# Queries of latent attention projected for two heads and two token tiles a step

## The reference, cut to what matters

```python
def mla_mixer(h, positions, w_in, q_a_norm, kv_a_norm, w_q_b, w_kv_b, q_norm, k_norm, w_out):
    b, s, _ = h.shape
    proj = h @ w_in
    cq = rms_norm(proj[..., :Q_LORA], q_a_norm)                     # 384 wide
    ckv = rms_norm(proj[..., Q_LORA:Q_LORA + KV_LORA], kv_a_norm)   # 256 wide
    k_rope = proj[..., Q_LORA + KV_LORA:]                           # 32 wide, one for all heads
    q = (cq @ w_q_b).reshape(b, s, MLA_HEADS, QK_DIM)               # 64 nope + 32 rope a head
    kv = (ckv @ w_kv_b).reshape(b, s, MLA_HEADS, QK_NOPE + V_DIM)   # 64 key + 64 value a head
    q_nope, q_rope = q[..., :QK_NOPE], q[..., QK_NOPE:]
    k_nope, v = kv[..., :QK_NOPE], kv[..., QK_NOPE:]
    q_nope = rms_norm(q_nope, q_norm[:QK_NOPE])
    q_rope = rms_norm(q_rope, q_norm[QK_NOPE:])
    k_nope = rms_norm(k_nope, k_norm[:QK_NOPE])
    k_rope = rms_norm(k_rope, k_norm[QK_NOPE:])
    cos, sin = rope_cos_sin(positions)
    q_rope = apply_rope(q_rope, cos[:, :, None], sin[:, :, None])   # x1*cos - x2*sin, x2*cos + x1*sin
    k_rope = apply_rope(k_rope, cos, sin)
    o = causal_block_attention(q_nope, q_rope, k_nope, k_rope, v)
    return o.reshape(b, s, MLA_HEADS * V_DIM) @ w_out
```

## Time and profile before

| | |
|---|---|
| Median of 3 runs | 2739.85 us (2738.59 to 2742.94) |
| The profiled execution's own time | 2739.83 us |
| Its span in the trace | 2738.6 us |
| TensorE busy | 2669.8 us, 97% of the span |
| DVE, ScalarE, POOL busy | 1608.3, 857.6, 665.7 us |
| Chain that ended last, by engine | PE 31%, DVE 5%, ACT 2%, issue 1%, POOL 1%, DMA 1% |

### The profile page before, as it was taken

The page is one execution under the profiler, slowest core; times in us unless marked ns, Lnnn a source line. Parts: engine busy times, 40 slices in busy tenths (PEclk is TensorE's granted clock), DMA queues, the critical chain, the costliest instruction groups (busy, mean ns, idle before and its releaser), DMA issues. The chain is left out here.

```text
span 2738.6 us, 33114 instructions
## 1 busy us (share of the span) xinstructions
PE 2669.8 (97%) x12932; PEld 2200.0 (80%) x12932; DVE 1608.3 (59%) x2366; ACT 857.6 (31%) x1485; POOL 665.7 (24%) x726
## 2 busy tenths in 40 slices
PE   8999999999999999999999999999999999899998
PEld 7888887787778888888888789878888878777776
DVE  5343468888746545555455556644443467768875
ACT  2101126676511001111011245521001035537885
POOL 2111121221321211221111258712111131012220
PEclk9999999999999999999999999999999999999999
DMA  4333333333235435444354400023333454048995
GB/s 126 98 95 100 93 98 110 94 104 95 79 102 152 140 114 145 117 137 140 115 147 130 151 17 1 1 72 98 99 94 100 93 68 72 8 140 287 349 357 218
DMA packets 456847, 325.84 MB, mean 119 GB/s; under 512 B 34434, under 2 KB 420819, under 8 KB 456435
## 3 DMA queue, kind: packets, MB, share of 16 engines
q1 hardware_dynamic: 434568, 282.77, 35.4%
q10 hardware_dynamic: 15498, 32.54, 3.7%
q0 software_dynamic: 6624, 8.41, 0.9%
HBM read 323.06 MB, written 16.32 MB: 124 GB/s over the span
## 5 line engine op out<-in xcount | busy, mean ns | idle before, releaser
L254 PE MATMUL bank<-h_hi,w_hi 128*128 128x512 f32 x1992 | 790.2, 397 | 8.9 <-DVE w_lo L246 4.4
L256 PE MATMUL bank<-h_hi,w_lo 128*128 128x512 f32 x1992 | 776.2, 390 | 0.0
L255 PE MATMUL bank<-h_lo,w_hi 128*128 128x512 f32 x1992 | 775.8, 389 | 0.0
L232 POOL TENSOR_SCALAR w_hi<-w_lo_exact 128x1024 fp32r<-128x1024 f32 x325 | 358.1, 1102 | 1483.0 <-DMA w_lo_exact<-in_ffn_w_gate 386.3
L246 DVE TENSOR_TENSOR w_lo<-w_lo_exact,w_hi 128x1024 fp32r<-128x1024 f32 x369 | 454.9, 1234 | 143.0 <-POOL w_hi L232 131.3
L254 PEld LDWEIGHTS bank<-h_hi,w_hi 128*128 128x128 f32 x1992 | 374.3, 188 | 95.5 <-ACT h_hi L350 6.8
L255 PEld LDWEIGHTS bank<-h_lo,w_hi 128*128 128x128 f32 x1992 | 374.5, 188 | 79.6 <-issue 3.6
L256 PEld LDWEIGHTS bank<-h_hi,w_lo 128*128 128x128 f32 x1992 | 374.2, 188 | 79.0
L254 PE MATMUL bank<-g_hi,w_hi 128*128 128x512 f32 x704 | 273.9, 389 | 0.0
L255 PE MATMUL bank<-g_lo,w_hi 128*128 128x512 f32 x704 | 273.9, 389 | 0.0
L256 PE MATMUL bank<-g_hi,w_lo 128*128 128x512 f32 x704 | 273.9, 389 | 0.0
(11 more groups left out here) (492 smaller groups left out, 3873.3 us busy)
## 6 DMA issues: line engine op xcount, KB each, us to landing
w_lo_exact<-in_ffn_w_gate SPq DMA_DIRECT2D x88, 512.0 KB, 3.8
w_lo_exact<-in_ffn_w_up SPq DMA_DIRECT2D x88, 512.0 KB, 3.9
w_lo_exact<-in_ssm_w_in SPq DMA_DIRECT2D x48, 512.0 KB, 4.1
mod_w<-in_w_mod ACTq DMA_DIRECT2D x48, 512.0 KB, 3.8
e_lo_exact<-in_w_gate SPq DMA_DIRECT2D x46, 512.0 KB, 5.7
e_lo_exact<-in_w_up SPq DMA_DIRECT2D x46, 512.0 KB, 6.7
e_lo_exact<-in_w_down SPq DMA_DIRECT2D x46, 512.0 KB, 5.9
w_lo_exact<-in_ffn_w_down SPq DMA_DIRECT2D x32, 512.0 KB, 4.0
```

The source lines that it names most:

```text
L232: ge.tensor_scalar(k.w_hi[:, u % SLOTS, :], k.raw[:, u % SLOTS, :], 1.0, 0.0, ALU.mult, ALU.add).then_inc(*k.up("w hi", u))
L254: te.matmul(k.bank[bank][:, :], hi, x_hi, start=first, stop=False)
L255: te.matmul(k.bank[bank][:, :], hi, x_lo, start=False, stop=False)
L256: return te.matmul(k.bank[bank][:, :], lo, x_hi, start=False, stop=stop)
```

## The change

Five edits in the latent attention stage:

- A query projection no longer covers one head and four token tiles, but two heads and two token tiles: six products of 192 columns in place of twelve of 96. There are still 16 of them, called s here; s = 0 and 1 are heads 0 and 1 (tiles 0 and 1, then 2 and 3), s = 2 and 3 heads 2 and 3, and so on. A head needs both of its pair's, so queries run one step further ahead: in step h, s = h+3. The lead-in does s = 0, 1 and 2. The normalised queries have two buffers, the second in a slot of the weight ring, whose load (the fourth unit of the projection out) waits until the last query is turned.
- The gains of the query's and key's nope part become one column, their product. It multiplies the query when it is turned: ScalarE's high part takes it as a scale, DVE's low part as the scalar of a SCALAR_TENSOR_TENSOR. Two DMAs of 96 single elements load it.
- The gains of the query's rope part go into four copies of the rotation's tables, `turns`, made once by POOL (`mla_tables_pool`, eight instructions).
- POOL's two gain multiplications a head (L2048, L2049) are gone; its rotation stays.
- Sums and normalisation run over i = -1 to 15: index i handles the key of head i and the query projection i+1.

```diff
@@ mla_tiles
+    k.base = k.ring_at + late_out_unit(k) % SLOTS * UNIT * 4
+    k.qc.append(sb("qc", [P, NT, 2, QK]))
+    k.turns = k.nr[:, :].rearrange("p (n a c) -> p n a c", n=4, a=2 * NT)
+    k.q_banks = [by_tile(k.bank[b][:, 0:NT * QK], NT) for b in (0, 3)]
@@ mla_sync
     for u in range(k.unit_at["mla"], k.unit_at["ffn11"]):
+        if u == late_out_unit(k):
+            k.se.wait_ge(*k.at("turned q", MLA_HEADS - 1))
         load_unit(k, u)
@@ mla_tensor
-    mla_project_tensor(k, 0, "q")
+    mla_queries_tensor(k, 0)
     te.wait_ge(*k.at("latent scaled", ("kv_a", LK - 1)))
-    mla_project_tensor(k, 0, "kv")
+    mla_keys_tensor(k, 0)
     mod_sum_tensor(k, 4, 14)
-    mla_project_tensor(k, 1, "q")
-    mla_project_tensor(k, 1, "kv")
+    mla_queries_tensor(k, 1)
+    mla_queries_tensor(k, 2)
+    mla_keys_tensor(k, 1)
     mla_turn_tensor(k, 0)
@@ in the loop over h
         if h + 2 < MLA_HEADS:
-            mla_project_tensor(k, h + 2, "q")
-            mla_project_tensor(k, h + 2, "kv")
+            if h + 3 < MLA_HEADS:
+                mla_queries_tensor(k, h + 3)
+            mla_keys_tensor(k, h + 2)
@@
+def mla_queries_tensor(k, s):
+
+    te = k.te
+    if s >= 2:
+        te.wait_ge(*k.at("normal", (s - 2, "q")))
+    for t in range(2):
+        tt, out = 2 * (s % 2) + t, q_bank(k, s)[:, 2 * t:2 * t + 2, :].rearrange("p a b -> p (a b)")
+        for m in range(LQ):
+            ins = te.matmul(out, k.latent[:, m, span(tt)], k.wq[:, m, s // 2 * 2 * QK:(s // 2 + 1) * 2 * QK], start=m == 0, stop=m == LQ - 1)
+    ins.then_inc(*k.up("projected q", s))
@@ mla_turn_tensor
-        te.wait_ge(*k.at(name + "c", h))
+        if name == "k":
+            te.wait_ge(*k.at("normal", (h, "kv")))
+            te.wait_ge(*k.at("kc", "rope"))
+        else:
+            te.wait_ge(*k.at("qc", h // 2 * 2 + 1))
@@ mla_scalar, lead-in
+    for n, name in enumerate(("mla_q_norm", "mla_k_norm")):
+        ae.dma_start(k.gain_col[:, n:n + 1], d[name].rearrange("a h -> h a")).then_inc(*k.up("load gain columns", "all", 16))
...
     mla_query_scalar(k, 0)
+    mla_inverse_scalar(k, -1, 2 * NT, NOPE)
+    mla_query_scalar(k, 1)
     mla_keys_scalar(k, 0)
     mla_inverse_scalar(k, 0, 3 * NT, NOPE)
-    mla_query_scalar(k, 1)
+    mla_query_scalar(k, 2)
     mla_keys_scalar(k, 1)
@@ mla_turn_scalar
-        ae.copy(t[:, 0, :], k.bank[TURN_BANKS[b]][0:QK, :]).then_inc(*k.up(name + "t hi", h))
+            ae.activation(t[:, 0, :], k.bank[TURN_BANKS[b]][0:QK, :], ACT.Copy, scale=k.gain_col[:, 2:3]).then_inc(*k.up("qt hi", h))
@@ mla_turn_vector
+            ve.scalar_tensor_tensor(t[:, 1, :], k.bank[TURN_BANKS[b]][0:QK, :], k.gain_col[:, 2:3], t[:, 0, :].bitcast(F32), ALU.mult, ALU.subtract).then_inc(*k.up("qt lo", h))
@@ mla_sums_vector
+    ve, s = k.ve, i + 1
+    if i >= 0:
+        ve.wait_ge(*k.at("sq k", i))
+    ve.wait_ge(*k.at("rr", i - 1 if s else "k rope"))
+    if s < MLA_HEADS:
+        ve.wait_ge(*k.at("sq q", s))
...
@@ mla_normalise_vector
+    ve.wait_ge(*k.at("rr", i))
+    if s < MLA_HEADS:
+        if s >= 4:
+            ve.wait_ge(*k.at("turned q", s // 2 * 2 - 3))
...
+    if i >= 1:
+        ve.wait_ge(*k.at("turned k", i - 1))
@@ mla_normalise_pool, gone
-    ge.tensor_tensor(k.qc[:, :, :], k.qc[:, :, :], k.gain[:, 0, :].unsqueeze(1).broadcast_to([P, NT, QK]), ALU.mult).then_inc(*k.up("qc", (h, 0)))
-    ge.tensor_tensor(k.kc[:, :, 0:NOPE], k.kc[:, :, 0:NOPE], k.gain[:, 1, 0:NOPE].unsqueeze(1).broadcast_to([P, NT, NOPE]), ALU.mult).then_inc(*k.up("kc", h))
```

More of the change, by code:

```diff
@@ L1868, in mla_vector @@
     mla_frequencies_vector(k)
+    mla_gain_vector(k)
     ve.wait_ge(*k.at("inverse rms", "mla"))
@@ L1891, in mla_vector @@
     mla_scaled_vector(k, "kv_a", LQ, LK)
-    for h in range(2):
-        mla_sums_vector(k, h)
-        if h:
+    for i in range(-1, 2):
+        mla_sums_vector(k, i)
+        if i == 1:
+            ve.wait_ge(*k.last("gain column"))
             mla_turn_vector(k, 0)
-        mla_normalise_vector(k, h)
+        mla_normalise_vector(k, i)
     for h in range(MLA_HEADS + 1):
@@ L1937, in mla_scaled_vector, with mla_gain_vector @@
         ve.scalar_tensor_tensor(k.latent[:, k0 + m, :], k.latent[:, k0 + m, :], k.col(name, m), k.latent_r[name], ALU.mult, ALU.mult).then_inc(*k.up("latent scaled", (name, m)))
+def mla_gain_vector(k):
+    ve = k.ve
+    ve.memset(k.gain_col[NOPE:QK, 2:3], 1.0).then_inc(*k.up("gain column", 0))
+    ve.wait_ge(*k.at("load gain columns", "all"))
+    ve.tensor_tensor(k.gain_col[0:NOPE, 2:3], k.gain_col[0:NOPE, 0:1], k.gain_col[0:NOPE, 1:2], ALU.mult).then_inc(*k.up("gain column", 1))
 def mla_frequencies_vector(k):
@@ L2017, in mla_pool @@
     split_pool(k, u0 + LQ + LK + 1, u0 + LQ + LK + 3)
-    mla_rotate_pool(k, k.kr[:, :, :], k.kc[:, :, NOPE:QK], "kc", "rope", k.at("unit", u0 + LQ + LK))
+    mla_rotate_pool(k, k.kr[:, :, :], k.kc[:, :, NOPE:QK], [t[:, :, :] for t in (k.cos, k.sin, k.cos, k.sin)], "kc", "rope")
+    mla_tables_pool(k)
     for half in range(2):
@@ L2021, in mla_pool @@
             fill_pool(k, values[:, half, :, n, :], 0.0, "vn")
-    mla_normalise_pool(k, 0)
-    mla_normalise_pool(k, 1)
+    for s in range(3):
+        mla_queries_pool(k, s)
     for h in range(MLA_HEADS):
```

119 lines of the change are left out of this document (69 added, 50 removed).

## The result

The changed kernel takes 2741.19 us (median of 14 runs, 2738.22 to 2744.73), the kernel before beside it 2739.35 (2736.03 to 2742.94). The ratio is 1.0014, interval 1.0007 to 1.0020: slower by a small amount, where 2738.0 and "no change" were forecast. The profiled execution took 2743.49 us, 2742.2 of it the span.

What follows compares the result with a forecast made beforehand. TensorE, busy 97% of the span, was taken as the bound. 2739.83 + 6.8 (lead-in) + 0.4 (DMAs) - 7.4 (steps 0 to 12) - 1.6 (step 13) = 2738.0 us; own range 2735 to 2741, 8 in 10 2733.5 to 2743.

Steps and rivals of the forecast that it cites:

- The pass: Loop's query projections: a 192-column pass takes 0.168 us, twelve take 2.01 us, gaining 0.64 us a projection.
- the line between 128 and 512: Interpolation between float32 passes of 128 columns (0.114 us) and 512 (0.4375 us), giving 0.168 us for 192.
- The gain column: Loop steps: DVE's low part of the query, now with a column, takes 0.07 us more, paid each step.
- step 13: Loop step carrying only keys now: falls from 11.26 us to about 9.7, 1.6 us less.
- The lead-in: Ahead of the loop: TensorE waits about 3.3 us before query 2; head 0 starts 6.8 us late, slow clock included.
- The clock term: Lead-in: clock falls at the 3.3 us stop, low until about 1606, losing 2.8 us; bounds 0 and 4.2.
- The two cases of the earlier trace: TensorE waits of 3.50 and 2.53 us in this stage, both with the clock falling from 2.4 to 1.2 GHz.
- low for long: Rival, lead-in: clock stays low 10.2 us as in the second earlier case, 1.4 us more, 2739.4 us; chance 13%.
- The DMAs: Stage's start: two more DMAs on ScalarE ahead of `wq` and `wkv` add 0.4 us, bounds 0 and 0.9.
- Clock stays up: Rival, lead-in: the clock does not fall at the stop, 2.8 us less, 2735.2 us; chance 15%.
- step not shorter: Rival, loop: step stays 11.27 us as another wait, likeliest ScalarE's weights and squares, replaces PE's work; 2745.4 us; chance 7%.
- pass not cheaper: Rival, loop: a 192-column pass takes 0.221 us, as two of 96, so nothing is gained; 2746.3 us; chance 5%.

Runs made afterwards that it cites:

- pad_late: Changed kernel with already met waits on TensorE's queue in the experts' stage behind the mixer (368 more instructions): 2737.69 us, ratio 0.9995.
- pad128: Changed kernel with already met waits on TensorE's queue in the feed-forward stage ahead of the mixer (114 more instructions by the page): 2736.22 us, ratio 0.9994.
- after: The changed kernel as first measured against the kernel before: 2741.19 us, ratio 1.0014.
- after_again: The changed kernel once more, unchanged: 2742.01 us, ratio 1.0009 to the kernel before.
- early_q1: Changed kernel with query projection 1 issued directly behind query projection 0, ahead of the keys: 2736.17 us, ratio 0.9986.
- before: The kernel without the change, timed beside the changed one: 2739.35 us.
- before_again: The kernel before once more, unchanged, as a control: 2737.84 us, ratio 0.9998.
- before_pad128: Kernel before with the same already met waits in the feed-forward stage ahead of the mixer: 2737.84 us, ratio 0.9998.
- before_short: Kernel before without the third product of each expert's gate and up projection (368 instructions, behind the mixer); leaves work out, no time given; mixer 157.0 us.
- nogain_late: The kernel padded by 368 instructions in the experts' stage, with the nope gain column left out of what is computed: 2738.56 us, ratio 1.0000.
- pad_long: Changed kernel with more met waits on TensorE's queue in the experts' stage (736 more instructions by the page): 2740.99 us, one run.
- early_pad128: Changed kernel with query projection 1 directly behind projection 0, plus met waits in the feed-forward stage ahead of the mixer: 2731.65 us, ratio 0.9973.
- pad_scalar: Changed kernel with met waits on ScalarE's queue in the experts' stage, nothing more on TensorE's: 2744.58 us, one run.
- whole_loads: Changed kernel with the mixer's four query tiles loaded in 512-byte rows instead of two halves of 256-byte rows (other queries result): 2736.83 us, ratio 0.9997.
- narrow: Changed kernel with each query product of 192 columns issued as two of 96: 2745.08 us, ratio 1.0023.

## Why the prediction was wrong

The sum had 2738.0 us, 1.8 less than before. The changed kernel takes 2741.19, 1.8 more than the kernel before beside it: just past the forecast's own range of 2735 to 2741, inside the wider one of 2733.5 to 2743, and on the other side of no change. With its TensorE program at the old length (`pad_late`) it takes 2737.69, with the shorter padding (`pad128`) 2736.22. The step that failed is one that the prediction took without saying it: that **all stages but the changed one stand**, so that 2739.83 can be their base. The removed instructions shortened TensorE's program by two fetches. With that the mixer's 256-byte loads went from 30.6 to 40.6 ns a packet, a unit came 4.7 us later, and the mixer took about 7 us more: 160.4 to 161.4 in `after`, `after_again` and `early_q1`, 153.0 to 154.7 in `before`, `before_again` and `before_pad128`. No rival named it. The timed loss is smaller than these 7 us: the ratio is 1.0014 and 1.0009 for the changed kernel and 0.9994 and 0.9995 for `pad128` and `pad_late`, 4 to 5.5 us.

How much of the 7 us is shown? The late unit costs 3.4 us in the stretch: 1.7 by the wait (`before_short`, clock up) and as much by the low clock behind it. The wait's part comes with every program of 102 fetches that has these loads, and with no other. Some 2 us more lie in "behind", where the order of ScalarE's and DVE's work decides when the next scores start; `after`, `after_again` and `early_q1` have them, but so do `nogain_late` and `pad_long`, which have fast packets, and `early_pad128`. Slow loads bring them on, it seems, and are not their only cause. That is open, and with it why `pad_long` has the fastest packets and a mixer of 156.8.

About 1 us more stands at the mixer's very end and is hardly a loss. In `after` the granted clock falls there (a mean of 0.83 from 2345 to 2354.99, in `before` 1.00 from 2342 to 2350.5). Eight of the sixteen profiles have this fall, `before_pad128` among them, and in these the stretch from the next norm to the one after takes 15.0 us, in the other eight 16.3. Counted to that later norm, the three profiles of the change are 6.1 us behind the three of the kernel before (175.8 and 169.7 in the mean).

The terms, from profiles of all runs whose attention stage is that of before (4: `before`, `before_again`, `before_pad128`, `before_short`) or after (7: `after`, `after_again`, `pad128`, `pad_late`, `pad_scalar`, `pad_long`, `whole_loads`), mean of each:

| part of the stage | before | after | measured | forecast |
|---|---|---|---|---|
| norm to first scores | 51.1 | 57.2 | +6.2 | +7.2 |
| first scores to projection out | 185.7 | 176.8 | -8.9 | -9.0 |
| projection out to the next norm | 55.0 | 54.5 | -0.4 | 0 |
| sum | 291.8 | 288.5 | -3.2 | -1.8 |

- **The pass.** 0.163 us instead of 0.168, at the lower bound, which was worked out as 192 times 0.4375/512 = 0.164. So a float32 pass of 192 columns is already paced by its columns, and the line between 128 and 512 was the wrong interpolation. From the scores to the end of the key projection a step loses 0.72 us (7.84 before, 1658.54 - 1651.42 = 7.12 after), where I had 0.64. Right in kind.
- **The gain column.** 0.06 us where 0.07 was forecast. But from the key projection's end to the scores the step grew by 0.27, from 3.43 to 1662.24 - 1658.54 = 3.70. The other 0.2 us stand at DVE's small scaling of the sums. DVE, kernel before:

```profile
1656.82 0.32 DVE L1985 TENSOR_SCALAR ss<-ss 128x4 f32<-128x4 f32 x1
1656.90 0.42 DVE L1565 TENSOR_TENSOR turned_lo<-bank,turned_hi 128x256 fp32r<-128x256 f32 x1
```

and changed kernel:

```profile
1660.13 0.44 DVE L2051 TENSOR_SCALAR ss<-ss 128x4 f32<-128x4 f32 x1
1660.48 0.41 DVE L1565 TENSOR_TENSOR turned_lo<-bank,turned_hi 128x256 fp32r<-128x256 f32 x1
1660.81 0.67 DVE L2076 TENSOR_TENSOR kt<-bank,kt 96x512 fp32r<-96x512 f32 x1
1661.41 0.73 DVE L2078 SCALAR_TENSOR_TENSOR qt<-bank,gain_col,qt 96x512 fp32r<-96x512 f32 x1
```

  The next instruction starts 0.35 us behind it instead of 0.08. Both times POOL is scaling weights meanwhile (L1533); in the lead-in, with POOL idle, the same instruction takes 0.17. That the two share something is an argument, no experiment here tested it. Step 10.82 instead of 10.7, step 13 at 9.72 as forecast (9.7). That the loop's -9.0 came out as -8.9 is in part luck. The kernel before has one longer step (its chain):

```profile
1703.68 2.66 PE bank L1483 x16
...
1715.75 2.67 PE bank L1483 x16
```

  It takes 12.07 us here and 12.08 or 12.09 in the other three profiles of the attention before; the changed kernel has 10.82 at that place. DVE's small scaling takes 0.62 us in it, the longest of the sixteen. The prediction read 11.27 into every step and left these 0.8 us out. Steps of 10.82 us and not 10.7 cost 1.5 us over thirteen of them; these 0.8 us make up for half of it, and small gains at steps 0, 13 and 14 for most of the rest.
- **The lead-in.** Wait 3.27 (3.3 forecast). From query 0 to the scores 21.32 us against 15.76 before, so +5.6; of that 1.6 is the slow clock (3.57 us for query 2 instead of 1.96) and 4.0 the rest, as forecast. The clock term was put at 2.8 and measured 1.6, since the clock came back 3 us after TensorE resumed and not 5.6. The clock falls at this place in each of the seven profiles of the change's own attention. The two cases of the earlier trace rows and this one differ more than I allowed for. The upper bound of 4.2 was also too small by its own figures: 10.2 us from 1599.5 end at 1609.7, which is 9.3 us behind 1600.4 and costs 4.65, so "low for long" stood at 2739.9 and not 2739.4.
- **The DMAs.** +0.4 forecast. No cost is seen: from the stage's norm to the sum of the first squares (the matmuls of `norm_acc` with `ones`) the kernel before takes 25.0 and 25.6 us where its clock stays up, the changed one 25.3 to 25.5 (three profiles).
- **Noise that I did not price.** That same stretch, ahead of query 0 and untouched by the change but for the DMAs, swings: 28.4 us in `before`, 25.0 in `before_again`, the same kernel. The clock makes the difference, with a mean of 0.88 over the stretch in one and 1.00 in the other. So the fall of the earlier trace rows at the 3.50 us wait, which I read as what a long wait does, comes in some executions and not in others: at the same place the clock fell at a wait of 2.96 us in `after` and stayed up at one of 3.22 in `after_again`. A single pair of profiles says little of a 2 us term. This pair's 6.4 us of gain in the stage against 3.2 in the mean is such a case.
- **The rivals.** "Clock stays up", "low for long", "step not shorter" and "pass not cheaper" are all refuted by rows. `narrow` shows that the last one would have cost as priced (8.9 us over `pad128`, 7.4 over `pad_late`, 8.3 forecast).

The lesson for the chances: of the 0.10 for "slower", none stood for an effect outside of the stage, though 0.2% of this kernel is 5.5 us and seven stages were left as they are. Nor is 0.2% the least that can be told: 14 executions of each kernel gave an interval of 1.0007 to 1.0020.

## What to carry to other kernels

A change that adds or removes many instructions is to be compared stage by stage, and the untouched stages first: where one of them moves, repeat the build with its length restored by waits that are already met (51 ns each in the trace, beside passes of 227 ns, so free here). A weight load in 256-byte rows is a weak spot whose speed can change without a change to its code; the unit that the ring brings just in time should not be one of these. Work moved into a lead-in is free only at a place where the next engine already has what it needs: two projections back to back beat one on each side of a chain of waits by 5.8 us here.
